# Four weight sums of the recurrence's value projection: from VectorE to GpSimd

## The reference

```
z = h @ w_in
qa, ka, va, qh, fz_f, fz_b, ih, gh, gate_a, gate_h = jnp.split(z, IN_OFFSETS, axis=-1)
...
v = iz.astype(jnp.float32).reshape(B, S, HGRN_HEADS, HGRN_VDIM)   # iz is ih: the recurrence's values
```

## Time and profile before

| | us |
|---|---|
| median of 3 runs | 1445.69 (1445.1 to 1446.63) |
| the profiled execution, its own time | 1445.97 |
| its span, first to last instruction | 1444.2 |
| PE busy in the span | 1434.5 (99%) |
| DVE busy | 901.3 (62%) |
| ACT busy | 667.9 (46%) |
| POOL busy | 23.4 (2%) |

### The profile page before, as it was taken

How to read it: one execution, slowest core, us unless ns; L and a number is a source line. 1 busy time by engine, 2 the same in 40 slices (tenths; PEclk the granted TensorE clock), 3 DMA queues, 4 the chain that set the end, 5 groups by cost and what they waited for, 6 DMA issues and landing times.

```text
span 1444.2 us, 21211 instructions
## 1 busy us (share of the span) xinstructions
PE 1434.5 (99%) x8104; PEld 1226.8 (85%) x8104; DVE 901.3 (62%) x1419; ACT 667.9 (46%) x1078; POOL 23.4 (2%) x43
## 2 busy tenths in 40 slices
PE   9999999999999999999999999999999999999998
PEld 7799999888898888888888888888889888888886
DVE  6888775435763555567866776754447555564975
ACT  5455555334533446555445654553445433232542
POOL 0000000000100000000000000000000000000000
PEclk9999999999999999999999999999999999999999
DMA  5332323324232222226332222223331243323763
GB/s 198 117 118 93 112 89 117 123 96 132 87 115 92 86 80 77 74 65 189 97 94 69 71 76 69 73 74 119 115 102 44 89 146 102 97 92 115 242 184 130
DMA packets 44317, 153.71 MB, mean 106 GB/s; under 512 B 5287, under 2 KB 5287, under 8 KB 44240
## 3 DMA queue, kind: packets, MB, share of 16 engines
q1 hardware_dynamic: 41472, 143.67, 31.1%
q0 software_dynamic: 2624, 8.95, 2.0%
q10 hardware_dynamic: 144, 0.04, 0.0%
HBM read 147.63 MB, written 4.23 MB: 105 GB/s over the span
## 4 chain that ended last, share of the span: by engine, by line
PE 96%; DVE 2%; DMA 1%; ACT 1%; issue 0%; SPq 0%; DVEq 0%; ACTq 0%
PE ps L450 21%; PE ps L451 21%; PE ps L452 21%; PE ps L602 4%; PE ps L603 4%; PE ps L604 4%; PE ps L1650 2%; PE ps L1652 2%; PE ps L1651 2%; PE ps L2483 1%; PE ps L2047 1%; PE ps L2048 1%; PE ps L2049 1%; PE ps L2865 1%; PE ps L2463 1%; PE ps L2885 1%
## 5 line engine op out<-in xcount | busy, mean ns | idle before, releaser
L450 PE MATMUL ps<-hh,whi 128*128 128x512 f32 x976 | 386.3, 396 | 1.3 <-DVE wlo L413 0.9
L451 PE MATMUL ps<-hl,whi 128*128 128x512 f32 x976 | 380.2, 390 | 0.0
L452 PE MATMUL ps<-hh,wlo 128*128 128x512 f32 x976 | 380.2, 390 | 0.0
L413 DVE TENSOR_TENSOR wlo<-raw,whi 128x1024 fp32r<-128x1024 f32 x172 | 210.5, 1225 | 249.7 <-ACT whi L408 249.6
L408 ACT ACTIVATE whi<-raw 128x1024 fp32r<-128x1024 f32 x172 | 181.8, 1057 | 383.7 <-PE ps L452 351.6
L450 PEld LDWEIGHTS ps<-hh,whi 128*128 128x128 f32 x976 | 183.1, 188 | 46.2 <-issue 5.1
L452 PEld LDWEIGHTS ps<-hh,wlo 128*128 128x128 f32 x976 | 183.2, 188 | 38.8
L451 PEld LDWEIGHTS ps<-hl,whi 128*128 128x128 f32 x976 | 183.3, 188 | 36.2 <-issue 0.2
L450 PE MATMUL ps<-ah,whi 128*128 128x512 f32 (+1 forms) x192 | 71.6, 373 | 1.0 <-DVE wlo L413 1.0
L452 PE MATMUL ps<-ah,wlo 128*128 128x512 f32 (+1 forms) x192 | 71.3, 371 | 0.0
L451 PE MATMUL ps<-al,whi 128*128 128x512 f32 (+1 forms) x192 | 71.3, 371 | 0.0
(11 more groups left out here) (565 smaller groups left out, 2975.5 us busy)
## 6 DMA issues: line engine op xcount, KB each, us to landing
raw<-in_wstream SPq DMA_DIRECT2D x192, 512.0 KB, 3.5
w_raw<-in_wstream SPq DMA_DIRECT2D x32, 512.0 KB, 4.2
ring<-in_wstream SPq DMA_DIRECT2D x20, 512.0 KB, 4.4
xt<-in_x_t SPq DMA_DIRECT2D x16, 256.0 KB, 4.3
raw_sum<-in_wstream SPq DMA_DIRECT2D x8, 512.0 KB, 4.5
raw_direct<-in_wstream SPq DMA_DIRECT2D x4, 512.0 KB, 4.4
x_dram<-x_tok POOLq DMA_DIRECT2D x4, 512.0 KB, 4.1
x_tok<-x_dram POOLq DMA_DIRECT2D x4, 512.0 KB, 5.6
```

What stands on the lines that cost most here:

```text
L413: nc.vector.tensor_tensor(wlo[:, s, :], raw[:, s, :], whi[:, s, :].bitcast(F32), ALU.subtract).then_inc(split_done, 1)
L450: nc.tensor.matmul(out, w, m, start=start, stop=False)
L451: nc.tensor.matmul(out, w, ml, start=False, stop=False)
L452: return nc.tensor.matmul(out, wl, m, start=False, stop=stop)
```

## The change

GpSimd makes the four sums of chunk 1 (blocks 10 to 13), with a semaphore of its own, `late_sum`. VectorE keeps the four sums of chunk 0. The heads and tails of blocks 10 to 13 wait on `late_sum`; the counts of `s_sum` in later stages go down by four. Loads, matmuls and buffers are as before.

```diff
-AFTER_IH_S_SUM, AFTER_IH_T_SUM = IN_S_SUM + 8, IN_T_SUM + 4
+AFTER_IH_S_SUM, AFTER_IH_T_SUM = IN_S_SUM + 4, IN_T_SUM + 4
...
+        def ih_summed_at(m):
+
+            n = m - IH_DIRECT
+            return (sem("s_sum"), IN_S_SUM + n + 1) if n < 4 else (sem("late_sum"), n - 3)
+
         def ih_head(act, m):
 
             if m >= IH_DIRECT:
-                act.wait_ge(sem("s_sum"), IN_S_SUM + m - IH_DIRECT + 1)
+                act.wait_ge(*ih_summed_at(m))
...
             n = m - IH_DIRECT
             if n >= 0:
-                dve.wait_ge(sem("s_sum"), IN_S_SUM + n + 1)
+                dve.wait_ge(*ih_summed_at(m))
...
+        def ih_sums_pool(pool):
+
+            w22, w21, w11, w12 = (IH_DIRECT + 4 + i for i in range(4))
+            pool.wait_ge(*ih_landed(w22))
+            pool.wait_ge(*ih_landed(w21))
+            nc.gpsimd.tensor_tensor(ih_raw(w22), ih_raw(w22), ih_raw(w21), ALU.add).then_inc(sem("late_sum"), 1)
+            pool.wait_ge(*ih_landed(w11))
+            pool.wait_ge(sem("late_sum"), 1)
+            nc.gpsimd.tensor_tensor(ih_raw(w21), ih_raw(w21), ih_raw(w11), ALU.add).then_inc(sem("late_sum"), 1)
+            pool.wait_ge(sem("late_sum"), 2)
+            nc.gpsimd.tensor_tensor(ih_raw(w11), ih_raw(w11), ih_raw(w22), ALU.add).then_inc(sem("late_sum"), 1)
+            pool.wait_ge(*ih_landed(w12))
+            pool.wait_ge(sem("late_sum"), 3)
+            nc.gpsimd.tensor_tensor(ih_raw(w12), ih_raw(w12), ih_raw(w11), ALU.add).then_inc(sem("late_sum"), 1)
...
             ih_tail(dve, m + 1)
             m += 4
-            ih_sum(dve, m)
             ih_tail(dve, m - 2)
-            ih_sum(dve, m + 1)
-            ih_sum(dve, m + 2)
             ih_tail(dve, m - 1)
-            ih_tail(dve, m)
-            ih_sum(dve, m + 3)
-            for n in range(1, 4):
+            for n in range(4):
                 ih_tail(dve, m + n)
...
+            ih_sums_pool(pool)
             with pool.Fori(0, GH_HEADS) as h:
```

## The result

The changed kernel takes 1455.06 us (median of 6, 1454.63 to 1455.33) where the kernel before takes 1445.62 us beside it: 1.0063 times as long (95% interval 1.0052 to 1.0074), 9.44 us more. The prediction said 1454.0 us, in a range of 1445.0 to 1457.0.

A forecast was written before the change was run, and what follows sets the result against it. PE bounds the kernel, with DVE as full ahead of block 7. Four turns of 2.15 us cost 8.6 us, less block 9's 0.35 us: +8.25 us, forecast 1454.0 us, range 1445.0 to 1457.0.

The forecast's parts named there:

- What bounds the kernel, and the gain: PE is busy 99% of the span; DVE is as full from 685.0 to 704.7 us; gain at most 0.35 us.
- block 9's gap: PE loses 0.35 us at block 9 because tail(9) stands behind sum(11) and sum(12); the change removes this.
- block 7's gap: PE loses 0.26 us at block 7, waiting for tail(7); this stays, since sum(9) and tail(7) still stand.
- The price of a GpSimd sum: On POOL, two operands of 1024 read one after the other: 2.15 us a sum, with ends 1.12 and 2.44.
- The library load: On POOL, the ISA row ahead of the sums runs near 545 us with 145 us of cover; costed at nothing.
- The turns: POOL sums and DVE instructions with two SBUF operands wait out each other; tail(7) and block 7 come 8.6 us late; chance 0.56.
- The rival that DVE keeps the way: POOL's first sum waits for DVE's result sums, delaying sum(9) and block 7 by 1.0 us; +0.65 us, 1446.3 us; chance 0.12.
- the first turn: POOL's first sum starts near 690.6 us, so sum(7) on DVE starts at 692.8 us where it started at 690.80.
- The clock, the term that was mis-sized: PE's clock might fall to 1.2 GHz in waits ahead of blocks 5 and 6: 2.72 us for one block, range only.

The follow-up runs named there:

- The fills: The changed kernel, but GpSimd fills the four blocks with a constant instead of adding; 1445.48 us, 0.9998 times the kernel before.
- the library load alone: The kernel before plus one tiny GpSimd addition (128x16) that brings the library load, all eight sums on VectorE; 1446.06 us beside 1446.03.
- one read: The changed kernel, but each of GpSimd's four sums is a copy of one block; 1448.17 us, 1.0014 times the kernel before.
- the kernel with TensorE kept busy: The changed kernel with 15 more 128x512 matmuls on TensorE ahead of blocks 5 and 6 each; 1454.07 us, 1.0058 times the kernel before.
- operands from PSUM: The changed kernel, but sum(7), tail(5), sum(8) and tail(6) on VectorE take their second operand from PSUM; 1451.69 us, 1.0039 times the kernel before.
- the first half's sums: GpSimd makes the sums of blocks 6 to 9, VectorE those of 10 to 13, against the changed kernel's split; 1447.51 us, 1.0011 times the kernel before.

## Why the prediction was right, point by point

**What bounds the kernel, and the gain.** Right. DVE was full in this stretch and PE waited for it. The fills, which take the sums off DVE and put no reads on GpSimd, gave 0.37 us: block 9's gap went, and block 7's stayed. (In the changed kernel block 7's gap of 0.26 us is gone too, since PE reaches block 7 later than tail(7) does.)

**The price of a GpSimd sum.** The prediction took 2.15 us from the copy's row as the sum's length and let DVE wait for all of it. The sum's length is 2.40 us where nothing holds it, and it holds DVE for 2.16 us of that. So the two operands are read one after the other, as assumed, but that the cost agrees to 0.01 us is in part luck: a sum longer than assumed, and a hold shorter than the sum. The estimate of 2.25 us, half of the figure that the Trainium skill gives for 2048 elements (GPSIMD Engine Reference, section 3.1), lies between these two. The library load was put at nothing, rightly: the first sum starts with its data. The 6 us that the same page (section 2.1) gives for a first call after a load does not show in these runs; the first addition behind the load (128x16, the library load alone) took 0.25 us and started 0.09 us after the row ahead of it.

**The turns.** Right, and now shown: the DVE starts are 3.29 to 3.31 us apart; with the second operand in PSUM, or with GpSimd only writing, the turns vanish, and with one read they shrink to 0.85 us. This agrees with the rule of the Trainium skill (SBUF — State Buffer, Who interferes with whom), down to the writes that do not count. Tail(7) was forecast 8.6 us late; counted from the stage's start it is 8.54 us late (705.86 - 697.68, plus 0.36 us by which the stage began earlier). The rival that DVE keeps the way falls: GpSimd gets in after each DVE instruction. Which of the two has the first turn was open, and the forecast gave it to GpSimd by a margin of 0.2 us (690.6 us against sum(7) at 690.80). So it fell in the changed kernel's trace; in that of the kernel with TensorE kept busy VectorE had it, and tail(7) came 0.89 us earlier. On this point the forecast had luck.

**The clock, the term that was mis-sized.** The forecast's sum had none for it and kept up to 2.72 us for the range. The clock fell in both waits, slowing block 5 by 1.52 and block 6 by 1.65 us. The first lay under the wait for tail(6), which is why that wait is 2.36 us and not some 4 us; of the second 0.91 us shows ahead of block 7. So block 7 begins when the slowed block 6 ends, 0.91 us after it could have begun behind tail(7), and not, as I wrote, with tail(7). This and the 0.4 us outside the span, which was not in the sum either, are 1.3 us; less some 0.1 us by which the turns were shorter than forecast and block 7, with no gap of its own, ran up faster, they make up the 1 us between 1454.0 and 1455.06 to within what the kernel's times scatter.

## What to carry to other kernels

An addition or copy moved from VectorE to GpSimd (here 128x1024, float32) does not run beside VectorE's instructions with two SBUF operands: each waits out the other's reads, so in this kernel a sum of 1.13 us taken off VectorE cost it 2.16 us of waiting. Before such a move, look at what VectorE does in that stretch, at its operands and at what is queued behind the instruction that would be held; GpSimd only writing, or VectorE's second operand in PSUM, cost VectorE nothing here. Where a queue is full, first ask whether its order is right: by the rows of the stage, two tails put ahead of two sums gave 0.66 us, more than the 0.35 us that the move was worth at best.

## What the runs showed that I had not expected

A DVE instruction that is held shows it as length (3.36 us in the place of 1.22), with no idle time ahead of it; who reads only the waits would take DVE for slower. PE's clock stood at 1.2 GHz after waits of 3.58 us (operands from PSUM) and 4.04 us, and again after one of 2.36 us behind block 5, whose first matmuls had been slow; after waits of 1.7 us and less (the first half's sums, one read) it was granted at 1.00. With the load and four further instructions on GpSimd the time lies some 0.4 us further above the span, for a reason that these runs leave open.
